# State-space pairs of a two-block transformer kernel: weight sums issued earlier, a separate place for one half tile, and ScalarE's copies in another order

## What is computed

```
z, xbc, dt_raw, ... = jnp.split(h @ w_in, IN_SPLITS, axis=-1)
xbc = jax.nn.silu(causal_depthwise_conv(xbc, ssd_conv_w) + ssd_conv_b)
xs, Bm, Cm = jnp.split(xbc, [SSD_INNER, SSD_INNER + SSD_GROUPS * SSD_STATE], axis=-1)
CB = jnp.einsum("bclgn,bcsgn->bcgls", Cc, Bc)
scores = CB[:, :, :, None] * Lmat                 # Lmat: exp of segment sums, causal
y_diag = jnp.einsum("bcgrls,bcsgrp->bclgrp", scores, X)
y = y_diag + y_off + D * xg                       # y_off from the running state
```

## Time and profile before

| | us |
|---|---|
| median of 3 runs | 3140.13 (3139.86 to 3147.58) |
| the profiled execution, its own time | 3139.91 |
| span of the profiled execution | 3138.3 |
| TensorE busy | 3020.8 (96%) |
| VectorE busy | 1876.8 (60%) |
| ScalarE busy | 571.6 (18%) |
| GpSimd busy | 314.2 (10%) |
| mean granted TensorE clock | 0.987 |

### The profile page before, as it was taken

The page is one execution under the profiler, slowest core; times in us unless marked ns, Lnnn a source line. Parts: engine busy times, 40 slices in busy tenths (PEclk is TensorE's granted clock), DMA queues, the critical chain, the costliest instruction groups (busy, mean ns, idle before and its releaser), DMA issues. The chain is left out here.

```text
span 3138.3 us, 40652 instructions
## 1 busy us (share of the span) xinstructions
PE 3020.8 (96%) x12895; PEld 1816.6 (58%) x12896; DVE 1876.8 (60%) x3950; ACT 571.6 (18%) x1318; POOL 314.2 (10%) x429
## 2 busy tenths in 40 slices
PE   7999999999999899999998998999999999999998
PEld 5767888744447433333333445478744688588543
DVE  5766887666456544333433477575657655665667
ACT  1002333210012122222221225410000233200000
POOL 1011122011100222222212100000000000000000
PEclk9999999999999999999999999999999999999999
DMA  7663232489753579999997421122245324132342
GB/s 257 187 209 112 76 101 61 148 257 300 246 186 133 201 309 387 368 395 377 392 363 269 172 81 54 41 101 81 108 161 180 91 74 140 46 101 81 142 180 107
DMA packets 267915, 570.83 MB, mean 182 GB/s; under 512 B 27050, under 2 KB 162837, under 8 KB 241931
## 3 DMA queue, kind: packets, MB, share of 16 engines
q1 hardware_dynamic: 210784, 415.82, 37.3%
q0 software_dynamic: 46992, 140.43, 12.8%
q10 hardware_dynamic: 10010, 12.92, 1.2%
HBM read 556.32 MB, written 38.93 MB: 190 GB/s over the span
## 5 line engine op out<-in xcount | busy, mean ns | idle before, releaser
L1647 PE MATMUL ps<-WR,hT 128*64 x832 | 374.1, 603 | 22.4 <-issue 20.9
L1648 PE MATMUL ps<-WR,hT 128*64 128x512 f32 x832 | 374.1, 603 | 0.0
L2092 PE MATMUL ps<-WR 128*128 128x512 f32 x784 | 337.4, 592 | 1.0 <-DVEq L3763 0.7
L1647 PEld LDWEIGHTS ps<-WR,hT 128*64 128x64 f32 x832 | 115.3, 139 | 264.9 <-issue 264.9
L2092 PEld LDWEIGHTS ps<-WR 128*128 128x128 f32 x784 | 148.6, 190 | 188.9 <-issue 186.1
L3475 DVE COPY WR<-WR 128x1024 f32 x208 | 131.0, 693 | 158.0 <-SPq L805 106.7
L2051 PE MATMUL ps<-WR 128*128 128x256 f32 x960 | 217.0, 379 | 0.0
L2051 PEld LDWEIGHTS ps<-WR 128*128 128x128 f32 x960 | 182.4, 190 | 24.8
L1668 PE MATMUL ps<-WR 128*64 x416 | 189.5, 598 | 2.8 <-DVEq L3488 1.8
L1669 PE MATMUL ps<-WR 128*64 128x512 f32 x416 | 189.6, 598 | 0.0
L3809 DVE TENSOR_TENSOR WR<-ps,WR 128x256 f32<-128x256 f32 x210 | 86.0, 423 | 145.1 <-PE ps L2051 143.2
(11 more groups left out here) (505 smaller groups left out, 5007.6 us busy)
## 6 DMA issues: line engine op xcount, KB each, us to landing
WR<-in_w_gate SPq DMA_DIRECT2D x64, 1024.0 KB, 8.7
WR<-in_w_up SPq DMA_DIRECT2D x64, 1024.0 KB, 11.1
WR<-in_w_down SPq DMA_DIRECT2D x64, 1024.0 KB, 10.2
WR<-in_mlp_w SPq DMA_DIRECT2D x56, 1024.0 KB, 6.7
WR<-in_mlp_w SPq DMA_DIRECT2D x20, 2048.0 KB, 8.5
xr<-in_ada_w POOLq DMA_DIRECT2D x32, 1024.0 KB, 5.7
WR<-in_w_in SPq DMA_DIRECT2D x56, 512.0 KB, 7.5
xr<-in_w_ada POOLq DMA_DIRECT2D x16, 1024.0 KB, 5.7
```

Of the source, the lines that this page charges most:

```text
L1647: mm(out[0:HALF], xT[u][:, k, 0:HALF], wa[:, :, k, :], start=(k == 0), stop=(k == KD - 1))
L1648: last = mm(out[HALF:P], xT[u][:, k, HALF:P], wb[:, :, k, :], start=(k == 0), stop=(k == KD - 1))
L2092: return mm(ps[:, bank, :], rows, weights, start=(row == 0), stop=(row == PAST[phase] - 1))
```

## The change

The first half of pair h = 1 gets a place of its own: `pair_x` becomes one list per pair, and the tile that c1 and u2 of the pair h = 1 write is now `hexp[1]`, a 128x512 view of the buffer `dtw`, which is free in this stage. The other tile (c21, u3) is still shared. The semaphore counts change to match: c1 waits for the last reader of its own tile in the group before, u3 of the pair h = 1 for convolution 1. `ssd_corners` and `ssd_conv` read the same places. On ScalarE, c1 and c5 of the pair h = 1 go ahead of the tanh of tile 0, u2 and the exp of chunk 2 ahead of the tanh of tile 1, and the exp of chunk 3, with its DMA, ahead of c21. On GpSimd the sums of the first pair go ahead of the wait for `rows_T` and the two small DMAs to `gate_rows`. Nothing is added or removed on any engine; TensorE's and VectorE's orders are the same.

```
-        pair_x = [view(WR, 4096 + 3072 + T * r, T) for r in range(2)]
+        pair_x = [[view(WR, 4096 + 3072, T), view(WR, 4096 + 3072 + T, T)], [hexp[1], view(WR, 4096 + 3072 + T, T)]]
...
-            pool.wait_ge(sem("rows_T"), 1)
...
             pair_sums(1, 1)
+            pool.wait_ge(sem("rows_T"), 1)
+            for n, r in ((0, 0), (1, 24)):
+                pool.dma_start(gate_rows[n * KD:(n + 1) * KD], prow[r:r + KD, 0, :]).then_inc(sem("gate_out"), 16)
+            pool.wait_ge(sem("gate_out"), 32)
...
             def ssd_copies(p, h, *events):
-                read = 4 * (p - 1) + 2 if h == 0 else 4 * p
+                x = pair_x[h]
+                read = 4 * (p - 1) + 2 * h
...
                         act.wait_ge(*pair_p(q, "p7"))
-                        act.wait_ge(sem("ssd_conv"), read + 2)
-                        into, bank = pair_x[1][:, 2 * P:], r1
+                        act.wait_ge(sem("ssd_conv"), 4 * p - 2 + 2 * h + 2)
+                        into, bank = x[1][:, 2 * P:], r1
...
             def ssd_turn(p, c, f):
...
                     ssd_tanh(p, 0)
+                    ssd_copies(p, 1, "c1", "c5")
                 else:
...
                     ssd_copies(p, 0, "c21")
+                    ssd_copies(p, 1, "c1", "c5")
                     ssd_tanh(p, 0)
-                ssd_copies(p, 1, "c1", "c5")
-                ssd_tanh(p, 1)
                 ssd_copies(p, 1, "u2")
                 ssd_decays(2, c)
-                ssd_copies(p, 1, "u3", "c21")
+                ssd_tanh(p, 1)
+                ssd_copies(p, 1, "u3")
                 ssd_decays(3, c)
+                ssd_copies(p, 1, "c21")
                 ssd_tanh(p, 2)
```

More of the change, by code:

```diff
@@ L975, in _, with row, gains @@
             pair_sums(1, 1)
+            pool.wait_ge(sem("rows_T"), 1)
+            for n, r in ((0, 0), (1, 24)):
+                pool.dma_start(gate_rows[n * KD:(n + 1) * KD], prow[r:r + KD, 0, :]).then_inc(sem("gate_out"), 16)
+            pool.wait_ge(sem("gate_out"), 32)
+            def row(n):
+                return gate_rows[n * KD:(n + 1) * KD].rearrange("k p -> (k p)").partition_broadcast(P)
+            def gains(n, g, b, sem_name, count):
+                pool.wait_ge(sem(sem_name), count)
+                pool.dma_start(lngb[:, 0, :], g.partition_broadcast(P)).then_inc(sem("ln_in"), 16)
+                pool.dma_start(lngb[:, 1, :], b.partition_broadcast(P)).then_inc(sem("ln_in"), 16)
+                pool.dma_start(grow[:, :], row(n)).then_inc(sem("ln_in"), 16)
             for p in range(2, SSD_GROUPS):
@@ L2314, in ssd_copies @@
                         act.wait_ge(sem("ssd_conv"), read + 1)
-                        into, bank = pair_x[0][:, 0:2 * P], r1
+                        into, bank = x[0][:, 0:2 * P], r1
                     elif event == "c5":
@@ L2322, in ssd_copies @@
                         act.wait_ge(*pair_p(q, "p6"))
-                        into, bank = pair_x[0][:, 2 * P:], r1
+                        into, bank = x[0][:, 2 * P:], r1
                     elif event == "u3":
                         act.wait_ge(*pair_p(q, "p7"))
-                        act.wait_ge(sem("ssd_conv"), read + 2)
-                        into, bank = pair_x[1][:, 2 * P:], r1
+                        act.wait_ge(sem("ssd_conv"), 4 * p - 2 + 2 * h + 2)
+                        into, bank = x[1][:, 2 * P:], r1
                     else:
                         act.wait_ge(*pair_p(q, "p4"))
-                        into, bank = pair_x[1][:, 0:2 * P], r1
+                        into, bank = x[1][:, 0:2 * P], r1
                     A(into, ps[:, bank, 0:2 * P], ACT.Copy).then_inc(sem("seven_c"), 1)
@@ L2978, in ssd_conv @@
                     dve.wait_ge(*pair_v(q, "c22" if k % 2 else "c12"))
-                    x = pair_x[k % 2]
+                    x = pair_x[k // 2][k % 2]
                 else:
@@ L2992, in ssd_corners @@
                 q = pair_no(p, h)
-                c11, c12, c22 = pair_x[0][:, 0:2 * P], pair_x[0][:, 2 * P:], pair_x[1][:, 2 * P:]
+                x = pair_x[h]
+                c11, c12, c22 = x[0][:, 0:2 * P], x[0][:, 2 * P:], x[1][:, 2 * P:]
                 r1, r2, r3 = SSD_R
```

## The result

The changed kernel takes 3159.68 us (median of 7 runs, 3153.77 to 3162.48), the kernel before 3141.12 us in 7 runs beside them. The ratio, estimated from all 14 runs, is **1.0052**, 95% interval 1.004 to 1.0063: slower by 0.5% or 16.3 us (12.6 to 19.8). The two medians alone differ by 18.6 us. The forecast was 3155 us, slower, range 3130 to 3164. The profiled execution took 3157.06 us, its span is 3155.4 us, 17.1 us more than before.

The account below looks back on a forecast made before the run. TensorE, busy 96% of the span, was taken to bound the kernel. Five turns at +2.05 (+10.25), turn 6 at -1.63 and clock +6.7 gave +15.3 on 3139.91: 3155 us, range 3130 to 3164.

Parts of the forecast that it names:

- The gain at p6: TensorE's wait for c1 at p6 goes, putting it 2.05 us ahead per turn from p2 on.
- The meeting: GpSimd's sums start at 323.09, ahead of VectorE's segments 3, which end at 328.9 instead of 325.22; z starts at 330.37.
- alternation: GpSimd sums and VectorE's L3073 and four segments take turns, each waiting for the other's whole instruction; chance 0.6.
- rival 1: VectorE keeps the port for the four segments: z at 328.42, no clock loss, 3138.8 us; chance 0.2 together with rival 3.
- Rival 2: Sums and segments 3 don't meet, or the delay is covered: six turns gain 1.63 us each, 3130.1 us; chance 0.2.
- Rival 3: Stall at p6 stays because something else holds c1: time unchanged; chance 0.2 together with rival 1.
- The price of a late z: In turns c = 1 to 5, z waits about 3.9 us for c21, making each turn 2.05 us longer.
- Turn 6: Turn c = 6 has no further pair to sum for, so it gains 1.63 us.
- The clock: TensorE's clock falls after each 3.9 us wait at z: 0 to 2.68 us per turn, middle 1.34 taken.
- Rival 4: Engines alternate at segments 3 but TensorE's clock does not fall: +8.6 us, 3148.5 us; chance 0.1.
- The sum: Five longer turns +10.25, turn 6 -1.63, clock +6.7: together +15.3 us, 3155 us.
- At nothing: Earlier first sums, two small DMAs, new tile's address and turn c = 0 cost nothing; up to 5 us without TensorE's cover.

Follow-up runs that it names:

- with nothing else in the way: Changed kernel with c21 of pair 1 back ahead of segments 3, DMA and exp, and GpSimd's sums for pair 0 held until segments 3 end: ratio 0.9958.
- the kernel whose sums wait: Changed kernel, c21 left behind the exp, with GpSimd's sums for pair 0 of the next group held until segments 3 have ended: ratio 0.9967.
- c21 ahead: Changed kernel with c21 of pair 1 back ahead of segments 3, the DMA and the exp of chunk 3: ratio 0.9944, repeated 0.9952.
- spare work in the wait: Changed kernel with 8 unused spare products in front of z in turns c = 1 to 5: ratio 1.0013 against the kernel before.

## Why the prediction was right

**The gain at p6.** Forecast 2.05 us per turn, measured 2.06 (47.23 against 49.29 with nothing else in the way). Right.

**The meeting.** Forecast: sums 0.31 us behind p3, in front of L3073 and the segments; end of segments 3 at 328.9, z at 330.37. Measured 328.83 and 330.32, in a turn that started 0.12 later; within its turn z starts 1.88 us later than before (35.16 against 33.28), the forecast had 2.05. Right, and the step on which the forecast rested, alternation across four unseparated instructions, holds: VectorE did not keep its place (rival 1), with 4.04 us for the four. Rival 2's place is taken by the kernel whose sums wait: that is what the change would have done without a meeting. Rival 3 is out, since the waits at p6 went. A sixth wait of about 0.3 us in the turn c = 6 is not among the waits, but z starts 31.48 us into that turn, against 31.24 with c21 ahead.

**The price of a late z.** Forecast 2.05 per turn, measured 1.97 with spare work in the wait. Turn 6: forecast -1.63, measured -1.71.

**The clock.** This is the term that was mis-sized. I took the middle of 0 and 2.68 us, 1.34 per turn, 6.7 in all; the turns show 1.45 to 2.91, mean 2.42, 12.1 in all. The upper end, where the Trainium skill's page "TensorE: Matmul & The Clock Gate" (Part 1) put it, was nearer. That page has the clock fall after idle time as a rule, and all five waits of 3.8 us bear that out. Rival 4, alternation without clock loss, is out with it.

**The sum.** 5 x 1.97 - 1.71 + 12.1 = 20.2 for the stage instead of 15.3. Behind it 3.4 us came back by the clock, by chance; I had allowed 2 us either way there, but for transfers. So it is partly luck that 3155 lies within 2 us of the profiled execution (3157.06): two errors of opposite sign, and the stage alone would have given 3160. The ratio's 16.3 us over the kernel before lie between 15.3 and 20.2; in which of the others the clock fell where, no trace shows.

**At nothing.** The first sums, the two DMAs, the new tile and the turn c = 0 cost nothing that shows. For the sums the run with them alone has it (0.9997), for the tile the turn of 47.23 us, which keeps the whole gain of 2.06. For the turn c = 0 the evidence is weaker: turn 1 starts 0.12 us later in the changed kernel, but in the two executions of the kernel with c21 ahead it starts at 296.22 and at 292.11. That the kernel before would spread from 3129.6 to 3149.2 us over its later runs was not in my working; the comparisons are therefore made by ratio and by the turns of the traces.

## What to carry to other kernels

A wait that goes away moves everything behind it earlier, also the start of another engine's work, so ask what that work will now run beside: here two microseconds of lead set four GpSimd instructions against four short VectorE ones and turned 1.14 us into 4.04. An instruction that frees the busiest engine should not stand in a queue behind one that waits for something else, even if today that something is always done in time. And a new wait on TensorE costs its own length and can cost the clock after it; here that second part was the larger one (12.1 us, against 9.85 for the late starts themselves).

## What the runs showed of the hardware

- VectorE instructions with two inputs from SBUF and GpSimd instructions on SBUF take turns one by one, also within an unseparated row of the same engine: four instructions of 0.29 us each took 4.04 us beside sums of 1.3 us, the slowest one 1.35 us. The Trainium skill's page "SBUF — State Buffer", section "SBUF: two separate sides", has the lock per instruction, and the trace agrees; that neither engine keeps it over two instructions in a row while the other one waits is what the runs add.
- An idle time of 1.8 us was followed by a fall of the clock in two turns of five in front of z, behind chunk 2 with its eight small products (L1335, 64 columns), and in none of six in front of p6, behind full products of 256 columns. The length of the idle time alone does not tell. Nor do the products in front of it alone, since they were the same in all five turns; that they count too is suggested by the two cases, not shown.
- Keeping TensorE at work for 3.5 of the 3.8 us, with products that nobody reads, kept the clock at 1.00 in all five turns, where five waits of 3.8 us without them had it at 0.70 to 0.84.
